# One 512-column matmul for the high part and residual of x, in the 48 slots of the first block whose outputs are features

## The reference, cut to what matters

```python
u_lru, g_lru, q, k, v, g_attn, m_lru, m_attn = jnp.split(z, split_at, axis=-1)
u = centred_depthwise_conv(u_lru, conv_w[l], conv_b[l])
h = (rg_lru(u, ..., False) + rg_lru(u, ..., True))      # two scans over time, one reversed
y_a = h.astype(x.dtype) * jax.nn.silu(g_lru)
...
y_b = windowed_gqa(q, k, v, attn_sink[l]) * jax.nn.silu(g_attn)
merged = (jax.nn.sigmoid(m_lru) * (y_a @ w_proj_a[l]) + jax.nn.sigmoid(m_attn) * (y_b @ w_proj_b[l]))
x = x + rms_norm(merged @ w_out[l], norm_post_w[l])
```

## Time and profile before

| | |
|---|---|
| runs (median of 3) | 2003.69 us (2001.08 to 2004.81) |
| profiled execution | 2001.45 us, of which its span is 1999.7 us |
| mean granted TensorE clock | 0.995 |
| TensorE, VectorE, ScalarE busy | 97%, 63%, 55% of the span |

### The profile page before, as it was taken

One profiled execution on the slowest core, in us unless ns is written; L12 is line 12 of the kernel. 1 busy time (PEld: TensorE's weight loads), 2 busy tenths in 40 slices (PEclk: granted clock), 3 DMA queues, 4 the chain that ended last, 5 costly groups with the idle time before them and its releaser, 6 DMA issues.

```text
span 1999.7 us, 32635 instructions
## 1 busy us (share of the span) xinstructions
PE 1938.2 (97%) x13840; PEld 1729.1 (86%) x13840; DVE 1266.0 (63%) x1771; ACT 1105.4 (55%) x1506; POOL 70.5 (4%) x66
## 2 busy tenths in 40 slices
PE   6999999999999999999899999899999999999998
PEld 6999989999888888888798988888889998988887
DVE  5877755555444444654598987554557889775453
ACT  5877745544433333434556578726455656883451
POOL 0111100000000000000000011000000000010000
PEclk9999999999999999999999999999999999999999
DMA  6454454443455555564544343412555443332154
GB/s 219 188 189 171 149 213 169 148 149 147 171 187 193 195 183 192 187 252 168 205 174 163 132 166 113 144 65 95 214 201 210 178 149 132 130 145 86 64 191 147
DMA packets 52272, 328.61 MB, mean 164 GB/s; under 512 B 7968, under 2 KB 10144, under 8 KB 14368
## 3 DMA queue, kind: packets, MB, share of 16 engines
q1 hardware_dynamic: 52128, 326.54, 45.2%
HBM read 320.23 MB, written 6.29 MB: 163 GB/s over the span
## 4 chain that ended last, share of the span: by engine, by line
PE 27%; DVE 10%; ACT 8%; DMA 4%; issue 2%; SPq 0%; ACTq 0%; DVEq 0%
PE z L306 13%; PE z L318 5%; DMA w_raw<-in_w_dram 4%; DVE w_lo L277 4%; ACT w_hi L270 3%; PE aux L2679 2%; DVE acc L2008 2%; DVE conv L2166 1%; PE z L342 1%; PE aux L2595 1%; PE aux L2684 1%; PE z L2524 1%; DVE S L2122 0%; PE aux L2763 0%; DVE S L2147 0%
## 5 line engine op out<-in xcount | busy, mean ns | idle before, releaser
L277 DVE TENSOR_TENSOR w_lo<-w_raw,w_hi 128x2048 fp32r<-128x2048 f32 x274 | 631.4, 2305 | 442.6 <-ACT w_hi L270 442.1
L270 ACT ACTIVATE w_hi<-w_raw 128x2048 fp32r<-128x2048 f32 x286 | 547.5, 1917 | 512.8 <-PE z L318 251.6
L306 PE MATMUL z<-xn_hi,w_hi 128*128 128x256 f32 x2112 | 620.9, 294 | 4.3 <-DVE g_all L842 2.3
L306 PE MATMUL z<-xn_hi,w_lo 128*128 128x256 f32 x2112 | 597.6, 283 | 0.0
L306 PE MATMUL z<-xn_lo,w_hi 128*128 128x256 f32 x2112 | 597.0, 283 | 0.0
L306 PEld LDWEIGHTS z<-xn_hi,w_hi 128*128 128x128 f32 x2112 | 400.4, 190 | 20.9 <-issue 8.9
L306 PEld LDWEIGHTS z<-xn_lo,w_hi 128*128 128x128 f32 x2112 | 400.0, 189 | 5.0 <-issue 4.3
L306 PEld LDWEIGHTS z<-xn_hi,w_lo 128*128 128x128 f32 x2112 | 398.7, 189 | 0.0
L318 PE MATMUL z<-w_hi,xn_hi 128*128 128x512 f32 x568 | 226.9, 399 | 0.0
L318 PE MATMUL z<-w_lo,xn_hi 128*128 128x512 f32 x568 | 225.2, 396 | 0.0
L318 PE MATMUL z<-w_hi,xn_lo 128*128 128x512 f32 x568 | 225.1, 396 | 0.0
(11 more groups left out here) (428 smaller groups left out, 2530.6 us busy)
## 6 DMA issues: line engine op xcount, KB each, us to landing
w_raw<-in_w_dram SPq DMA_DIRECT2D x287, 1024.0 KB, 4.8
gate_w<-in_lru_w_dram SPq DMA_DIRECT2D x8, 512.0 KB, 5.0
x_t<-state_dram SPq DMA_DIRECT2D x2, 2048.0 KB, 8.4
x_first<-in_x_dram SPq DMA_DIRECT2D x4, 512.0 KB, 6.6
x_t<-in_x_dram SPq DMA_DIRECT2D x1, 2048.0 KB, 11.0
state_dram<-x_t SPq DMA_DIRECT2D x2, 1024.0 KB, 5.9
pw<-in_pw_dram SPq DMA_DIRECT2D x2, 1024.0 KB, 6.2
state_dram<-x_t SPq DMA_DIRECT2D x8, 256.0 KB, 2.3
```

The source lines that it names most:

```text
L270: act.activation(self.k.w_hi[:, n % SLOTS], self.k.w_raw[:, m % RAW], ACT.Copy).then_inc(self.s.rounded, 1)
L277: dve.tensor_tensor(self.k.w_lo[:, n % SLOTS], self.k.w_raw[:, m % RAW], self.k.w_hi[:, n % SLOTS].bitcast(F32), ALU.subtract).then_inc(se ...
L306: ins = pe.matmul(out, w[:, kk], x[:, kk], start=kk == 0 and j == 0, stop=kk == KT - 1 and j == 2)
```

## The change

x's high part and residual become one tile `xn` of shape 128 x 16 x 2 x 256: for each k-tile 256 columns of high part, then 256 of residual. A new function `wide_features` takes the place of `features` in the 48 slots. Per k-tile it issues one matmul of w_hi with all 512 columns and one of w_lo with the 256 of the high part. A PSUM bank then holds two halves, whose sum is the result. ScalarE copies the first half to SBUF and VectorE adds the second from PSUM (`join`), for u into `padded` at the head of `convolve`, for g_lru and g_attn into `g_all` and `gate`; the sigmoid and silu read the sum from SBUF. Semaphores `ujoined`, `gtaken`, `gjoined`, `ataken`, `ajoined` order this, and TensorE waits for the joins where it waited for the copies or products. Tiles that lie over x's (`junk`, `x_whole`) get the same stride.

```diff
+    def wide_features(self, pe, n, bank, x, each=None, whole=True):
+        w_hi, w_lo = (w[:, n % SLOTS].rearrange("p (k f) -> p k f", k=KT) for w in (self.k.w_hi, self.k.w_lo))
+        out = bank[:, 0:2 * T]
...
+            row = x[:, kk].rearrange("p b t -> p (b t)")
+            if kk < KT - 1:
+                pe.matmul(out, w_hi[:, kk], row, start=kk == 0, stop=False)
+            ins = pe.matmul(out[:, 0:T], w_lo[:, kk], x[:, kk, 0], start=False, stop=False)
+            if kk == KT - 1:
+                ins = pe.matmul(out, w_hi[:, kk], row, start=False, stop=True)
+        ins.then_inc(self.s.used, 1)
...
+                def take_gates(i):
+                    act.wait_ge(s.used, 4 * i + 4)
+                    if i:
+                        act.wait_ge(s.dsteps, 8 * i)
+                    for b in range(2):
+                        act.activation(g_all[:, b], tile(2 + b), ACT.Copy).then_inc(s.gtaken, 1)
+
                 def gate_inputs(i):
-                    act.wait_ge(s.used, 4 * i + 4)
                     if i:
                         act.wait_ge(s.zcopied, 2 * i)
                     for b in range(2):
-                        act.activation(gsig[:, b], tile(2 + b), ACT.Sigmoid).then_inc(s.gsig, 1)
+                        act.wait_ge(s.gjoined, 2 * i + b + 1)
+                        act.activation(gsig[:, b], g_all[:, b], ACT.Sigmoid).then_inc(s.gsig, 1)
...
                     if i:
-                        gate_inputs(i - 1)
+                        take_gates(i - 1)
                         gates(i - 1)
                     ring.round(act, n + 3)
                     if i:
+                        gate_inputs(i - 1)
                         tanhs(i - 1)
...
+                    take_gate(c, 0)
                     ring.round(act, n + 8)
+                    take_gate(c, 1)
+                    ring.round(act, n + 9)
                     silu(c, 0)
-                    ring.round(act, n + 9)
                     silu(c, 1)
-                    silu(c, 2)
+                    take_gate(c, 2)
                     ring.round(act, n + 10)
...
                 def convolve(i, b):
                     dve.wait_ge(s.ucopied, 2 * i + b + 1)
+                    inner = padded[:, b, 2:2 + T]
+                    dve.tensor_tensor(inner, rest(b), inner, ALU.add).then_inc(s.ujoined, 1)
+                    dve.wait_ge(s.ujoined, 2 * i + b + 1)
...
+                def join_gates(i):
+                    for b in range(2):
+                        dve.wait_ge(s.gtaken, 2 * i + b + 1)
+                        dve.tensor_tensor(g_all[:, b], rest(2 + b), g_all[:, b], ALU.add).then_inc(s.gjoined, 1)
...
-                        dve.tensor_tensor(g_all[:, b], tile(2 + b), gsig[:, b], ALU.mult).then_inc(s.zcopied, 1)
+                        dve.tensor_tensor(g_all[:, b], g_all[:, b], gsig[:, b], ALU.mult).then_inc(s.zcopied, 1)
...
                     if i:
-                        open_gates(i - 1)
+                        join_gates(i - 1)
                     ring.residual(dve, n + 3)
...
                         convolve(i, 0)
                         convolve(i, 1)
                     if i:
+                        open_gates(i - 1)
                         scan(i - 1)
...
                     ring.residual(dve, n + 7)
+                    join_gate(c, 0)
                     ring.residual(dve, n + 8)
                     soften(c, 0)
+                    join_gate(c, 1)
                     ring.residual(dve, n + 9)
                     soften(c, 1)
+                    join_gate(c, 2)
                     ring.residual(dve, n + 10)
...
                     for b in range(2):
                         if i:
-                            pe.wait_ge(s.zcopied, 2 * (i - 1) + b + 1)
-                        ring.features(pe, 4 * i + 2 + b, tile(2 + b), k.xn_hi, k.xn_lo)
+                            pe.wait_ge(s.gjoined, 2 * (i - 1) + b + 1)
+                        ring.wide_features(pe, 4 * i + 2 + b, z[2 + b], k.xn)
...
-        k.xn_hi, k.xn_lo = (put(n, [P, KT, T], F32R) for n in ("xn_hi", "xn_lo"))
+        k.xn = put("xn", [P, KT, 2, T], F32R)
+        k.xn_hi, k.xn_lo = k.xn[:, :, 0], k.xn[:, :, 1]
```

More of the change, by code:

```diff
@@ L307, in features @@
         ins.then_inc(self.s.used, 1)
+    def wide_features(self, pe, n, bank, x, each=None, whole=True):
+        w_hi, w_lo = (w[:, n % SLOTS].rearrange("p (k f) -> p k f", k=KT) for w in (self.k.w_hi, self.k.w_lo))
+        out = bank[:, 0:2 * T]
+        if whole:
+            self.await_slot(pe, n)
+        for kk in range(KT):
+            if each is not None:
+                each(kk)
+            row = x[:, kk].rearrange("p b t -> p (b t)")
[5 more added lines that the diff above has]
+        ins.then_inc(self.s.used, 1)
     def tokens(self, pe, n, quarter, outs, x_hi, x_lo):
@@ L445, in tile, with rest @@
             return z[n][:, 0:T]
+        def rest(n):
+            return z[n][:, T:2 * T]
         def pair(c):
@@ L668, in silu @@
                         act.wait_ge(yout[j // 2], c)
-                    act.activation(gate[:, j], tile(2 + j % 2), ACT.Silu).then_inc(s.silued, 1)
+                    act.activation(gate[:, j], tile(2 + j % 2), ACT.Copy).then_inc(s.ataken, 1)
+                def silu(c, j):
+                    act.wait_ge(s.ajoined, 4 * c + j + 1)
+                    act.activation(gate[:, j], gate[:, j], ACT.Silu).then_inc(s.silued, 1)
                 def finish_chunk(c, n):
+                    if c >= 0:
+                        take_gate(c, 3)
                     ring.round(act, n + 3)
@@ L678, in finish_chunk @@
                         copy_weights(c, 0)
+                        silu(c, 2)
                         silu(c, 3)
@@ L960, in normalise, with join_gate @@
                             dve.tensor_scalar(S[p][:, h, b], S[p][:, h, b], m[:, 0, i:i + 1], None, ALU.mult).then_inc(soft[p], 1)
+                def join_gate(c, j):
+                    dve.wait_ge(s.ataken, 4 * c + j + 1)
+                    dve.tensor_tensor(gate[:, j], rest(2 + j % 2), gate[:, j], ALU.add).then_inc(s.ajoined, 1)
                 def open_heads(c, p):
@@ L975, in finish_chunk @@
                         normalise(c, 0)
+                        join_gate(c, 3)
                     ring.residual(dve, n + 3)
@@ L1128, in _ @@
                         if i:
-                            pe.wait_ge(s.ucopied, 2 * (i - 1) + b + 1)
-                            ring.features(pe, 4 * i + b, tile(b), k.xn_hi, k.xn_lo)
+                            pe.wait_ge(s.ujoined, 2 * (i - 1) + b + 1)
+                        if i:
+                            ring.wide_features(pe, 4 * i + b, z[b], k.xn)
                         else:
-                            ring.features(pe, b, tile(b), k.xn_hi, k.xn_lo, (first_rows, second_rows)[b], False)
+                            ring.wide_features(pe, b, z[b], k.xn, (first_rows, second_rows)[b], False)
                     for b in range(2):
                         if i:
-                            pe.wait_ge(s.zcopied, 2 * (i - 1) + b + 1)
-                        ring.features(pe, 4 * i + 2 + b, tile(2 + b), k.xn_hi, k.xn_lo)
+                            pe.wait_ge(s.gjoined, 2 * (i - 1) + b + 1)
+                        ring.wide_features(pe, 4 * i + 2 + b, z[2 + b], k.xn)
                     gates(i)
-                pe.wait_ge(s.ucopied, 2 * LRU_PASSES)
+                pe.wait_ge(s.ujoined, 2 * LRU_PASSES)
                 for w in range(4):
@@ L1208, in _ @@
                         else:
-                            pe.wait_ge(s.silued, 4 * c + j - 1)
-                        ring.features(pe, n + 4 + j, tile(2 + j % 2), k.xn_hi, k.xn_lo)
+                            pe.wait_ge(s.ajoined, 4 * c + j - 1)
+                        ring.wide_features(pe, n + 4 + j, z[2 + j % 2], k.xn)
                         if j == 0:
@@ L1225, in _ @@
                     if c == 1:
[L1226 removed]
+                        pe.wait_ge(s.ajoined, 16)
                     elif c:
@@ L1931, in square @@
                 act.wait_ge(s.added, since.added + 2 * c + m + 1)
-                act.activation(k.junk[:, (2 * c + m) % 4 * Q:(2 * c + m) % 4 * Q + Q], x_t[:, m, cols(c)], ACT.Square, scale=D ** -0.5,
+                here = slice(2 * ((2 * c + m) % 4), 2 * ((2 * c + m) % 4) + 2)
+                act.activation(k.junk[:, here], x_t[:, m, cols(c)].rearrange("p (j t) -> p j t", t=T), ACT.Square, scale=D ** -0.5,
                                accum_out=k.squares[:, m, c:c + 1])
```

20 lines of the change are left out of this document (10 added, 10 removed).

## The result

The changed kernel takes 2008.94 us (median of 18 runs, 2006.15 to 2015.59) against 2004.64 us for the kernel before (18 runs taken beside them; one of these took 8869.29 us, like no other run of the study, and the ratio leaves it out). The ratio is 1.0026, with a 95% interval from 1.0018 to 1.0035: slower by 3.6 to 7.0 us. The forecast was 2008.2.

The account below looks back on a forecast made before the run. The prediction took TensorE's 26.49 us gate pass as the bound, 1.19 above the ScalarE-VectorE ring, which would take over at 27.39. +6.0 less 1.5 in attention gives +4.5 us: 2003.7 + 4.5 = 2008.2 us, range 1998 to 2014.

Parts of the forecast that it names:

- The ring: Gate passes: ScalarE and VectorE hand work in a circle, 25.30 us y to y, growing to 27.39, past TensorE's 26.12.
- the copies: Gate passes, ScalarE: two copies PSUM to SBUF between y and the gates add 0.54 us to the ring.
- the adds: Gate passes, VectorE: each convolve begins with an add from PSUM and waits for it, twice 0.44 = +0.88 us.
- `open_gates` 0.67: Gate passes, VectorE: moved from idle time to between convolve and scan, its two operations add 0.67 us.
- The start: Pass 0: VectorE's chain ends 0.88 us later, first join at 63.48, y at 84.35 instead of 80.60.
- The end of the gates: Gates of pass 7 at 239.6; split for slot 37 done at 272.45, TensorE waits 1.35 us; shift +6.0 us.
- The matmul's saving: Wide slots on TensorE: 0.0057 us saved per k-tile, up to 0.0131; in attention -1.5 us.
- The sum: Whole kernel: +6.0 us up to slot 37, less 1.5 in attention, is +4.5 us.
- TensorE as the bound (1): Gate passes: TensorE stays the bound if the ring gains less than 0.82 us; 1995 to 2001 us; chance 0.16.
- The wide matmul at 0.240 (2): Wide slots: 512 columns cost what two of 256 do, no saving, +6.0, 2009.7 us; chance 0.04.
- The token slots' pitch (3): Token slots: interleaved x moves some 1,700 matmuls between 0.2343 and 0.2269, 12.6 us either way; chance 0.06.
- The clock (4): Slot 37: a clock fall after the wait costs up to 2 us more, 2010; inside the forecast's range, no separate chance.

Follow-up runs that it names:

- early opening: Changed kernel with VectorE's open_gates moved ahead of the convolution, between the splits of n+3 and n+4: 2005.06 us, ratio 1.0000.
- the control: Kernel before with only the convolution's first half and ScalarE's copy for it moved ahead of round and split n+3: 2005.05 us, ratio 1.0003.
- the 32 bytes: Changed kernel with x 32 bytes lower, at an odd multiple of 64 bytes: 2002.79 us, ratio 0.9997 to the kernel before.
- gates wide only: Changed kernel with the wide matmul only in the 32 slots of the gate passes, attention as before: 2012.92 us, ratio 1.0045.
- attention wide only: Changed kernel with the wide matmul only in the 16 gate slots of the attention chunks, gate passes as before: 2006.69 us, ratio 1.0014.

## Why the prediction was right

**The ring, 25.30 + 0.54 + 0.88 + 0.67 = 27.39.** It measured 27.48. The three terms stand in the rows: the copies 0.54, the adds 2 x 0.45, `open_gates` 0.67. The early opening took exactly the last out, the control showed that no ring of 25.30 matters while TensorE needs 26.49, and the 32 bytes showed the reverse. Causes that would have done as well for the +4 us (VectorE's load, the layout, TensorE's reads) are each excluded by a run. So the mechanism was right. That the time came within 0.8 us (2008.94 for 2008.2) is in part luck, as the following shows.

**Two passes took 27.86 and 27.94.** In one ScalarE waited 0.70 us for a weight DMA, in the other 0.34; the ring has no slack to take it up. The prediction did not have this. The first of them comes back in other kernels: the same pass took 27.86 us with the gates wide only and 27.87 with x 32 bytes lower, with waits of 0.77 and 0.93 us for a DMA. Timeline of ScalarE:

```profile
130.55 1.92 ACT L270 ACTIVATE w_hi<-w_raw 128x2048 fp32r<-128x2048 f32 x1 [0.70 <-DMA w_raw<-in_w_dram]
```

**The start.** y of pass 0 was forecast at 84.35 and came at 83.30. I had let the join of g start at 63.48, 0.88 after `open_gates` of before; it started at 62.52. The longer wait ahead of gates 0 (2.32 for 1.42) was there, but TensorE reached them 0.98 earlier, in part because slots 0 to 3 are 0.6 us cheaper. This error, the two late DMAs (0.39 and 0.45 longer) and 0.09 us a pass of the ring nearly cancelled: gates 7 at 239.96 for 239.6.

**The end of the gates.** Split done at 272.85 for 272.45, TensorE's wait 1.21 for 1.35. The shift was forecast as 6.0 and measured 6.5 against the profile of before. Against the kernel before with the reorder, whose clock did not fall at slot 6, it is 7.9: heads turned 233.22 us from gates 0, against 225.30. The baseline was too slow by 1.4 us, because I took the one profiled execution as typical, though the clock rows showed what was in it.

**The matmul's saving** is the term that I mis-sized. I took 0.0057 us a k-tile of the two ends 0.0057 and 0.0131; it is 0.0094 to 0.0098, between them. That makes attention -2.3 instead of -1.5. The wide matmul costs 0.2323 and the narrow one 0.1179, so neither row was the price of the pair. By the rule of the Trainium skill (TensorE: Matmul & The Clock Gate, Back-to-back issue gap) the saving is estimated at 0.0025; the trace shows nearly four times that.

**The sum.** +7.9 - 2.3 = +5.6, which the first block shows as +5.7, and the ratio as +5.2. The forecast +4.5 had two errors of opposite sign, 1.9 too little at the gates and 0.8 too little saved. That they partly cancelled was luck: with the saving right and the gates as forecast it would have been +3.7.

**The rivals.** TensorE as the bound (1) is out: it waits 1.33 us in a pass. The wide matmul at 0.240 (2) is out: the pair takes 0.3502, not 0.360. The token slots' pitch (3) did not move with the layout, since x still began at the same place, but the suspicion behind it was worth more than the change: the place was the cause of nearly all of that 12.6 us (0.0073 of the 0.0074 us between the paces). The clock (4): after the wait of 2.57 us at slot 6 it stayed at 1.00, while before it had fallen after 2.28, so the length of the wait alone did not decide it. At the same place it stayed at 1.00 after 2.29 us with attention wide only, and after 2.30 us in the kernel before with x 96 bytes lower.

```profile
63.00:64.00 1.00, 1.00 (x5) 0.91 (x6) 1.00 (x2) 1.00 (x3) 0.00 (x0) 1.00 0.00 0
```

The window here is the one of the earlier trace rows that showed 0.50. At slot 37 the clock stayed up too.

## What to carry to other kernels

Where the busiest engine is full, look for the next circle of waits between the others and take its length from the trace, from one output to the same output a pass later. The difference between that and the busy engine's own time is the budget for any work moved to them; here it was 1.19 us a pass, and 2.1 us of small operations used it up. When the change also makes the busy engine's part shorter, the margin that keeps the whole gain is smaller: with a wide pass of 25.89 us it was 0.59.

Work added to an engine costs nothing in its idle time and its full time in the chain, so the place decides: the same adds cost 4 to 5 us in one order and let the kernel gain 5 in another. Look for the idle interval in the timeline before writing the edit.

Where two groups of equal instructions have different prices, ask about their addresses: one constant changed by 96 bytes was worth twice as much as the whole rework of the matmuls.

## What the hardware showed that was not expected

- The start address of an operand changed TensorE's pace by 2 to 3%. With x stationary: 0.2343 us at 96 mod 128, 0.2334 at 64 mod 128, 0.2270 at 0 mod 128. With x moving, 256 columns: 0.1200, 0.1178, 0.1200.
- A 512-column matmul with x moving and a 256-column one in turn take 0.2323 + 0.1179 us from start to start. The sum of 0.3502 is less than that of a token matmul on x and a 256-column matmul at the same address (0.2343 + 0.1200).
- The granted clock fell after a wait of 2.28 us in one kernel and not after one of 2.57 us at the same place in another. Two more kernels waited there 2.29 and 2.30 us without a fall.
